# Second products written back into PSUM banks, exponentials kept in banks, a chain of small table operations moved to GpSimd, and one weight load issued a stage earlier

## The reference, cut to what matters

```python
proj = _rmsnorm(h, norm_mix_g) @ w_in              # q, k, v (512 wide each) and u (512)
att  = _chunked_attention(_rmsnorm(q), _rmsnorm(k), v, rel_bias)   # the "band": softmax over a band, 8 heads
# state space (S5): per group of 16 channels 64 complex states
mag = exp(lr * step); ar = mag * cos(li * step); ai = mag * sin(li * step)
fr = (zr * lr + ai * li) / den;  fi = (ai * lr - zr * li) / den     # den = lr^2 + li^2
_, _, xr, xi = lax.associative_scan(_complex_affine_combine, (a_r, a_i, bu_r, bu_i), axis=1)
y = xr @ c_re - xi @ c_im + d_skip * u
y = gelu(y);  y = y * sigmoid(y @ w_glu + b_glu)    # the gated unit
mixed = concat(rmsnorm(att), rmsnorm(ssm)) @ w_out
```

## Time and profile before

| | |
|---|---|
| Median of 3 runs | 5517.76 us (5517.52 to 5522.59) |
| The profiled execution | 5523.01 us, its span 5521.2 us |
| PE / DVE / ACT / GpSimd busy over the span | 92% / 55% / 31% / 11% |
| DVE by fortieths of the span | 7574647888403444... |
| TensorE clock by fortieths | 9688999999999999... |

### The profile page before, as it was taken

One profiled execution on the slowest core, in us unless ns is written; L12 is line 12 of the kernel. 1 busy time (PEld: TensorE's weight loads), 2 busy tenths in 40 slices (PEclk: granted clock), 3 DMA queues, 4 the chain that ended last, 5 costly groups with the idle time before them and its releaser, 6 DMA issues. The chain is left out here.

```text
span 5521.2 us, 62480 instructions
## 1 busy us (share of the span) xinstructions
PE 5064.5 (92%) x23936; PEld 4048.4 (73%) x23936; DVE 3045.5 (55%) x5495; ACT 1729.4 (31%) x2614; POOL 634.6 (11%) x402
## 2 busy tenths in 40 slices
PE   7778899999998999988899998999888999989998
PEld 6227678888887888867877675788778876767787
DVE  7574647888403444465555565544555465566433
ACT  3303423333322322232233332333322233323421
POOL 0750002222240000001200001000012100011000
PEclk9688999999999999998999998999989999989998
DMA  2002123555545555520022120322200221212222
GB/s 100 0 23 77 62 92 121 182 178 180 173 146 209 190 191 196 193 94 11 1 88 80 35 86 30 106 92 96 84 31 1 74 70 56 69 42 96 88 96 73
DMA packets 231590, 525.49 MB, mean 95 GB/s; under 512 B 19584, under 2 KB 89472, under 8 KB 230016
## 3 DMA queue, kind: packets, MB, share of 16 engines
q1 hardware_dynamic: 231296, 521.51, 27.9%
HBM read 445.94 MB, written 75.50 MB: 94 GB/s over the span
## 5 line engine op out<-in xcount | busy, mean ns | idle before, releaser
L379 DVE TENSOR_TENSOR weight_low<-ring,weight_high 128x1024 fp32r<-128x1024 f32 (+2 forms) x622 | 725.8, 1167 | 1381.3 <-ACT weight_high L369 1380.4
L369 ACT CAST weight_high<-ring 128x1024 fp32r<-128x1024 f32 (+2 forms) x728 | 731.6, 1005 | 2112.8 <-PE banks L77 2102.4
L75 PE MATMUL banks<-x_high,weight_high 128*128 128x512 f32 x1856 | 753.6, 406 | 79.5 <-DVE x_low L428 32.8
L76 PE MATMUL banks<-x_low,weight_high 128*128 128x512 f32 x1856 | 732.6, 395 | 0.0
L77 PE MATMUL banks<-x_high,weight_low 128*128 128x512 f32 x1856 | 731.9, 394 | 0.0
L75 PEld LDWEIGHTS banks<-x_high,weight_high 128*128 128x128 f32 x1856 | 354.7, 191 | 195.0 <-issue 93.8
L75 PE MATMUL banks<-act_high,weight_high 128*128 128x512 f32 x1024 | 399.9, 391 | 16.8 <-DVE act_low L1701 16.8
L75 PE MATMUL banks<-xn_high,weight_high 128*128 128x512 f32 x1024 | 410.6, 401 | 0.7 <-ACT hT L1488 0.7
L76 PEld LDWEIGHTS banks<-x_low,weight_high 128*128 128x128 f32 x1856 | 354.7, 191 | 76.5 <-issue 5.8
L77 PEld LDWEIGHTS banks<-x_high,weight_low 128*128 128x128 f32 x1856 | 354.2, 191 | 76.1
L77 PE MATMUL banks<-xn_high,weight_low 128*128 128x512 f32 x1024 | 399.5, 390 | 0.0
(11 more groups left out here) (587 smaller groups left out, 9270.4 us busy)
## 6 DMA issues: line engine op xcount, KB each, us to landing
ring<-in_peer_u SPq DMA_DIRECT2D x128, 512.0 KB, 3.5
ring<-in_peer_v SPq DMA_DIRECT2D x128, 512.0 KB, 3.4
acts<-dot_act SPq DMA_DIRECT2D x128, 256.0 KB, 2.0
gates<-gate_block SPq DMA_DIRECT2D x64, 512.0 KB, 6.0
activations<-acts SPq DMA_DIRECT2D x128, 256.0 KB, 3.7
gates_in<-gates SPq DMA_DIRECT2D x128, 256.0 KB, 3.9
ring<-in_w_up SPq DMA_DIRECT2D x64, 512.0 KB, 3.2
ring<-in_w_down SPq DMA_DIRECT2D x64, 512.0 KB, 3.2
```

Source lines behind the costliest of these rows:

```text
L75: nc.tensor.matmul(out, w_high, x_high, start=start, stop=False)
L76: nc.tensor.matmul(out, w_high, x_low, start=False, stop=False)
L369: self.nc.scalar.copy(self.wH[:, g % 2, 0:kc * P], self.ring[:, g % SLOTS, 0:kc * P]).then_inc(self.high_made, 1)
L379: ops.tensor_tensor(self.wL[:, g % 2, 0:kc * P], self.ring[:, g % SLOTS, 0:kc * P], self.wH[:, g % 2, 0:kc * P].bitcast(F32), ALU.subtract ...
```

## The change

Four edits, all in the mixer.

1. **State space.** Before, DVE wrote all four products of the rotation to SBUF and added pairs of SBUF tensors. Now the two products with Ei are written back into the PSUM banks they come from, so each of the two sums has one operand in SBUF and one in PSUM. The count stays at six operations; fewer of them wait for the one just ahead.
2. **Band.** ACT writes the exponential into the score's bank instead of `pr`, DVE reads it there and writes the normalised row to `pr`. Two waits change their place with it.
3. **Tables.** The doublings, squarings, factors and 128x512 operations go from DVE to GpSimd's own list in the projection stage; DVE keeps one reciprocal, at i = 13. `scalar_tensor_tensor` steps become two instructions.
4. **Gated unit.** w_glu is loaded by SP during the state space stage, into `vS` (the values of the band, no longer read), and the stage's own buffer and wait go.

```diff
 # attention
+        def exps(j, w):
+            return score_banks[j % 3][:, 0:w] if in_banks else pr[:, j % 3, 0:w]
-                        pe.wait_ge(masked, j - 2)
+                        pe.wait_ge(normed if in_banks else masked, j - 2)
-                nc.vector.tensor_scalar(pr[:, j % 3, 0:w], pr[:, j % 3, 0:w], stats[:, 4 + j % 2:5 + j % 2], None,
+                if in_banks and j >= 3:
+                    dve.wait_ge(turned, j - 2)
+                nc.vector.tensor_scalar(pr[:, j % 3, 0:w], exps(j, w), stats[:, 4 + j % 2:5 + j % 2], None, ALU.mult).then_inc(normed, 1)
-                    if j >= 3:
+                    if j >= 3 and not in_banks:
                         act.wait_ge(turned, j - 2)
-                    nc.scalar.activation(pr[:, j % 3, 0:w], sc[:, j % 2, 0:w], ACT.Exp, bias=stats[:, j % 2:j % 2 + 1],
+                    nc.scalar.activation(exps(j, w), sc[:, j % 2, 0:w], ACT.Exp, bias=stats[:, j % 2:j % 2 + 1],
 # StateTables.dve_at: the code of i = 4 to 12 goes, this stays
+        if i == 13:
+            dve.wait_ge(self.squared, 1)
+            v.reciprocal(den, den).then_inc(self.inverse, 1)
 # StateTables.pool
+        pool.wait_ge(self.exps, 1)
+        pool.wait_ge(self.sines, 2)
...
+        g.tensor_tensor(den, den, tmp, ALU.add).then_inc(self.squared, 1)
...
+        for k in range(8):
...
+            link(g.tensor_tensor(s2_, s_, c_, ALU.mult))
+            link(g.tensor_scalar(s2_, s2_, 2.0, None, ALU.mult))
...
+        pool.wait_ge(self.inverse, 1)
+        link(g.tensor_tensor(fr, fr, den, ALU.mult))
+        link(g.tensor_tensor(fi, fi, den, ALU.mult))
+        pool.wait_ge(self.loaded, 64)
+        link(g.tensor_tensor(c1, cre, bc(fr, 32), ALU.mult))
+        link(g.tensor_tensor(c2, cim, bc(fi, 32), ALU.mult))
...
         pool.wait_ge(self.bias_loaded, 16)
 # state_space
+            for f in range(4):
+                sp.dma_start(glu[:, f, :], row(dram["w_glu"], f)).then_inc(glu_loaded, 16)
-                link(v.tensor_tensor(w[:, 0, :], b0, Er[:, i, :], ALU.mult))
-                link(v.tensor_tensor(w[:, 1, :], b1, Ei[:, i, :], ALU.mult))
-                link(v.tensor_tensor(w[:, 0, :], w[:, 0, :], w[:, 1, :], ALU.add))
-                link(v.tensor_tensor(w[:, 1, :], b1, Er[:, i, :], ALU.mult))
+                v.tensor_tensor(w[:, 0, :], b0, Er[:, i, :], ALU.mult)
+                v.tensor_tensor(w[:, 1, :], b1, Er[:, i, :], ALU.mult)
+                link(v.tensor_tensor(b1, b1, Ei[:, i, :], ALU.mult))
+                v.tensor_tensor(b0, b0, Ei[:, i, :], ALU.mult)
+                link(v.tensor_tensor(w[:, 0, :], w[:, 0, :], b1, ALU.add))
+                v.tensor_tensor(w[:, 1, :], w[:, 1, :], b0, ALU.subtract).then_inc(rotated, 1)
                 if i >= 2:
                     dve.wait_ge(products, i - 1)
-                v.tensor_tensor(w[:, 2, :], b0, Ei[:, i, :], ALU.mult).then_inc(rotated, 1)
                 dve.wait_ge(rotated, i + 1)
-                link(v.tensor_tensor(w[:, 1, :], w[:, 1, :], w[:, 2, :], ALU.subtract))
 # gated_unit
-                sp.dma_start(glu[:, f * 512:(f + 1) * 512], row(dram["w_glu"], f)).then_inc(loaded, 16)
-            pe.wait_ge(loaded, 64)
```

More of the change, by code:

```diff
@@ L763, in attention @@
 def attention(nc, name, heads, scores, keys, scale, bias, values, depth, place, out, banks, sc, pr, pt, stats, ident,
-              aside=None, beside=None, packed=False):
+              aside=None, beside=None, packed=False, in_banks=False):
     jobs = [(h, q) for h in range(heads) for q in range(TT)]
@@ L1005, in mix @@
                               lambda h: mixT[half(h), h // 2, :], banks, *attention_memory(scratch, ring, spare), ident,
-                              aside=ssm)
-                    state_space(nc, ssm, col, uT, banks, scratch, ring)
-                gated_unit(nc, dram, cols, uT, mixT, banks, scratch, Ahead(weights, dram["w_out"], 0))
+                              aside=ssm, in_banks=True)
+                    state_space(nc, dram, ssm, col, uT, vS, banks, scratch, ring)
+                gated_unit(nc, dram, cols, uT, mixT, vS, banks, scratch, Ahead(weights, dram["w_out"], 0))
                 with ExitStack() as out:
@@ L1073 @@
 class StateTables:
-    NAMES = "c_loaded step_done angles_ready exps_done sines_done dve_step bias_loaded"
+    NAMES = "c_loaded step_done angles_ready exps_done sines_done dve_step bias_loaded pool_step squared inverse"
     def __init__(self, nc, held, dram, col, cols, mixT):
@@ L1098, in take @@
     def take(self, sems):
-        self.loaded, self.step_done, self.angles, self.exps, self.sines, self.dve_step, self.bias_loaded = sems
+        self.loaded, self.step_done, self.angles, self.exps, self.sines, self.dve_step, self.bias_loaded, self.pool_step, self.squared, self.inverse = sems
     def loads(self, sp):
@@ L1121, in dve_at @@
     def dve_at(self, dve, i):
-        nc, power, cre, cim, c1, c2, cols = self.nc, self.power, self.cre, self.cim, self.c1, self.c2, self.cols
+        nc, cols = self.nc, self.cols
         step, lre, mag, sn, cs, tmp, turns, fr, fi, den, zr_, th, aim = (self.par[:, k, :] for k in range(13))
@@ L1132, in dve_at @@
             sine(nc, link, th, turns, self.turns_int[:], sn, cs).then_inc(self.angles, 1)
[L1133 to L1173, removed]
@@ L1176, in pool @@
         pool.wait_ge(self.bias_loaded, 16)
-        self.nc.gpsimd.memset(self.bias[0:64, :, 448:512], NEG)
+        g.memset(self.bias[0:64, :, 448:512], NEG)
     LAST = 8
@@ L1210, in act_aside, with state_space @@
                 self.nc.scalar.activation(E[:, t, n:2 * n], E[:, t, 0:n], ACT.Copy, scale=self.power[:, k, 0, t:t + 1]).then_inc(scaled, 1)
-def state_space(nc, tables, col, uT, banks, scratch, ring):
+def state_space(nc, dram, tables, col, uT, glu, banks, scratch, ring):
     N = SSM_TILES
@@ L1220, in state_space, with _ @@
     sets = [scratch[:], ring[:].rearrange("p s (two n) -> p (s two) n", two=2)]
-    with stage(nc, "b_ready turned_in scanned products y_ready y_summed y_activated dve_step pool_step") as (
-            block, b_ready, rotated, scanned, products, y_ready, summed, activated, dve_step, pool_step):
+    with stage(nc, "b_ready turned_in scanned products y_ready y_summed y_activated dve_step glu_loaded") as (
+            block, b_ready, rotated, scanned, products, y_ready, summed, activated, dve_step, glu_loaded):
+        @block.sync
+        def _(sp):
+            for f in range(4):
+                sp.dma_start(glu[:, f, :], row(dram["w_glu"], f)).then_inc(glu_loaded, 16)
+            sp.wait_ge(glu_loaded, 64)
         @block.tensor
@@ L1285, in _, with gated_unit @@
                 nc.scalar.activation(uT[:, g, :], uT[:, g, :], ACT.Gelu).then_inc(activated, 1)
-def gated_unit(nc, dram, cols, uT, mixT, banks, scratch, ahead):
+def gated_unit(nc, dram, cols, uT, mixT, glu, banks, scratch, ahead):
     bglu = cols("b_glu")
-    with ExitStack() as held, stage(nc, "glu_loaded glu_done gate_ready gated") as (block, loaded, done, gate, gated):
-        glu = held.enter_context(nc.sbuf_tensor("glu_weights", [P, 4 * 512], F32))
+    with stage(nc, "glu_done gate_ready gated") as (block, done, gate, gated):
         @block.sync
         def _(sp):
-            for f in range(4):
-                sp.dma_start(glu[:, f * 512:(f + 1) * 512], row(dram["w_glu"], f)).then_inc(loaded, 16)
             ahead.sp(sp)
@@ L1305, in _ @@
         def _(pe):
-            pe.wait_ge(loaded, 64)
             for f in range(4):
                 for c in range(4):
-                    last = nc.tensor.matmul(banks[f], glu[:, f * 512 + c * P:f * 512 + (c + 1) * P], uT[:, c, :],
+                    last = nc.tensor.matmul(banks[f], glu[:, f, c * P:(c + 1) * P], uT[:, c, :],
                                             start=(c == 0), stop=(c == 3))
```

34 lines of the change are left out of this document (33 added, 1 removed).

## The result

The changed kernel took 5481.6 us (median of 4 runs, 5479.3 to 5486.6), the kernel before 5517.64 beside it (4 runs). The ratio is 0.9935, 95% interval 0.9919 to 0.9950: 36 us faster where some 32 were forecast.

What follows compares the result with a forecast made beforehand. DVE was taken to bound the state space and nearly fill the projection, with GpSimd pacing much of the band. Savings of 17.9 + 5.8 + 0.7 + 7.7 = 32.1 us gave 5486 us against 5517.76, range 5468 to 5500.

Steps and rivals of the forecast that it cites:

- State space: Mixer's state space: DVE bounds it; tile period falls from 8.54 to 7.37 us, saving 17.9 us, the largest term.
- would wait as L1254 did: State space: the first scan, two SBUF inputs, waits for GpSimd's fourth product until 4.97 us into the tile; period 7.37.
- The rival of free scans: State space: scans don't meet GpSimd's lock; period 6.35 us, term 33.2, time 5470, likely 5473; 20%.
- Projection: Projection: without the tables on DVE, PE becomes the bound and GpSimd's tail ends last; 5.8 us saved, between 4 and 8.3.
- The rival of the wrong place for the tables: Projection: GpSimd's table operations stall DVE or are starved by its reciprocals; term 0, time 5492 or 5496; 12%.
- Band: Band: DVE's product leaves GpSimd's way, but the doublings and then ACT set the pace; 0.7 us, between -1 and 5.
- what is left is one head: Band: only one head gains, some 0.7 us twice on PE's path, less a slower read in the last head.
- savings before job 19 only lengthen ACT's wait there: Band: ACT waited 6.54 us at job 19 for GpSimd's doublings; savings in the first nineteen jobs only lengthen that.
- Gated unit: Gated unit: PE starts 6.7 us earlier without the w_glu wait, plus 1 of 3.1 us for the clock; 7.7 us.
- The slower rival: State space: PE's clock falls and PE bounds it; at 11.0 us per tile the time is 5540; 5%.
- One of its counter-arguments: Against a falling PE clock: where PE was full, the clock was 1.00; less idle time should lift it.

Runs made afterwards that it cites:

- Three products: Changed kernel with the third of GpSimd's four state space products left out, PE adding the fourth twice: 5470.6 us, state space stage 116.25 us.
- scans from banks: Changed kernel with the rotation's sums also written into the PSUM banks, so each scan reads one SBUF tensor and one bank: 5468.4 us, ratio 0.9909.
- filled band: Changed kernel with three more 128x128 identity matmuls per band job into unused bank 7, which nothing reads: 5482.2 us, ratio 0.9938.

## Why the prediction was right, point by point

**State space: right in mechanism and size, less a tail.** From the first rotation operation to the end of the last scan, DVE took 381.69 - 246.87 = 134.82 us before and 352.89 - 236.03 = 116.86 after: 18.0, against 17.9 forecast. The step that carried it was that the scans, which had never met GpSimd in the trace, would wait as L1254 did; period 7.37 us, forecast 7.37. Three products and the scans from banks confirm it. The stage gained 16.8. Its first projections were 0.5 us quicker, and its end 1.7 slower: PE's last matmuls (L1258) took 5.32 us at a clock of 0.68 instead of 3.62 at 1.00. In the changed kernel once more they took 3.62 at 1.00, and the stage gained 17.9.

**The rival of free scans**: false as stated, since 2.18 us were measured; the 6.35 us that it would have given is what DVE needs alone, and the scans from banks reach it (6.36). Their stage is 148.99 - 116.04 = 33.0 us shorter than before, the rival's term of 33.2.

**Projection: right.** GpSimd's tail was the new bound. Its end was forecast for 117.5 and came at 117.9; the two operations without a row took 1.49 us, the upper end of their bound, and the memset 0.52 of the 1.1 allowed for it. PE's pace of 6.35 us per tile held (98.55 - 92.19 = 6.36 for DVE's L379).

**The rival of the wrong place for the tables**: it named a real effect that was too small. Some of GpSimd's small operations waited beside L379 (1.28 us at 60.48, where its others take 0.22), but the part before the reciprocal was over at 69.6 us, and PE kept its pace.

**Band: mis-sized.** The forecast was 0.7 us, the profile shows 5.0, the means over executions differ by 2. The waits of DVE's product did go: its 32 instances take 17.6 us instead of 25.8 with the edit undone. What failed is the size in the step "what is left is one head": it counted instructions at fixed durations, while the last heads take 9.0 to 13.8 us from one execution to the next. It also put GpSimd's own gain, 0.6 us, at nothing. The forecast that savings before job 19 only lengthen ACT's wait there can't be judged from one pair of profiles, 4.63 us against 6.54. Over all of them the wait is 0.2 to 6.5 us with the exponentials in SBUF (mean 2.5) and 4.6 to 10.4 in banks (mean 7.7), so that step held. So did the direction and the bounds (-1 to 5), the upper one only just in the first profile: that the 5.0 came out so high is this execution's luck.

**Gated unit: right in mechanism, 7.7 forecast, 9.6 in the first profile and 8.1 in the others** (17.7 to 17.9 us). The wait was worth the 6.7. The rest was the clock, of which 1 of 3.1 us was counted; it stayed full in three of the eleven profiles of kernels with the load ahead. In the other eight the stage was 1.5 to 1.7 us longer.

**The slower rival** (PE bounds the state space at a falling clock) did not come up: the clock rose there, 0.78 to 0.82, and to 0.90 with the scans from banks, where PE was idle for 21.7 of 116 us and not for 36.4 of 149. One of its counter-arguments is weaker than it looked, though: PE full did not always go with a clock of 1.00, as the first 20 us of the filled band show (0.51).

**The sum.** By stages the profile missed the forecast by -0.5, +4.3, -1.1 and +1.9 us. The time came close in part because these are small against 32, and in part because two of them have the other sign; the two positive ones hang on the clock of the execution.

## What to carry to other kernels

Where DVE and GpSimd work side by side, count each DVE instruction's SBUF inputs: one operand of a two-input operation in a bank frees it of GpSimd, and writing an intermediate back into the bank that it came from costs nothing here (0.69 to 0.70 us). A tensor_scalar from SBUF to SBUF belongs on the list too; for it the bank has a price of 0.26 us at 512 columns, so it pays only where GpSimd is met. When such a wait is removed, look for the next two-input instruction in line, because the wait moves there (here from two additions to one scan). And work moved off a bound engine must also end before the stage's barrier: start it when its inputs are there, not where its old place in the loop was (2.9 us of the stage here, too little to see in the run). Last, a stage with idle PE time needs several profiles before a few us are put down to an edit: the band took 108.2 to 113.0 us with the same code.

## What was not expected of the hardware

- GpSimd's tensor_scalar on 128x512 takes 1.49 us, its tensor_tensor with a broadcast operand 1.05 and without one 1.26 to 1.29: the simpler operation is the slower one.
- A scan whose first input is a broadcast column in SBUF (2.18 us beside a product, 1.22 without) waits as an addition of two full operands does (1.78 and 0.69).
- DVE writes a bank in place in 0.69 to 0.70 us, as fast as it reads one.
- DVE's 3.34 us reciprocals (one SBUF input) did not hold up GpSimd's small operations beside them, which start at 63.37, 63.68, 64.02 and 64.31, the spacing of 0.3 us that they have elsewhere. DVE's product L837, also with one tensor from SBUF, does meet GpSimd (1.41 us for 0.49). What sets the two apart stays open here.
- PE full for 20 us at a granted clock of 0.51 at the start of the filled band, and at 1.00 in the next 20. What lets the clock rise there stays open.
